# A single-expert unit ahead of each group of mixed units, an early first weight load, and filler products, in a two-layer diffusion backbone with grouped experts

## What is computed

```python
x = x + gate2 * moe_ffn(rmsnorm(x) * (1 + scale2) + shift2)

def moe_ffn(h, ...):
    s = sigmoid(h @ w_router)                 # 16 experts in 4 groups of 4
    # best group by the sum of its two best biased scores, then its two best experts
    gates = the two chosen scores, divided by their sum
    hid = silu(h @ w1[e]) * (h @ w3[e])       # 1024 -> 256, for the chosen experts
    return sum over chosen e of gates[e] * (hid @ w2[e])    # 256 -> 1024
```

## Time and profile before

| | us |
|---|---|
| median of 3 runs | 1187.36 (1186.56 to 1190.74) |
| the profiled execution | 1180.08, its span 1177.2 |
| TensorE busy in it | 1094.7 |
| VectorE, ACT, POOL busy | 522.6, 275.8, 212.2 |

### The profile page before, as it was taken

How to read it: one execution, slowest core, us unless ns; L and a number is a source line. 1 busy time by engine, 2 the same in 40 slices (tenths; PEclk the granted TensorE clock), 3 DMA queues, 4 the chain that set the end, 5 groups by cost and what they waited for, 6 DMA issues and landing times.

```text
span 1177.2 us, 14999 instructions
## 1 busy us (share of the span) xinstructions
PE 1094.7 (93%) x5084; PEld 569.2 (48%) x5084; DVE 522.6 (44%) x1291; ACT 275.8 (23%) x637; POOL 212.2 (18%) x297
## 2 busy tenths in 40 slices
PE   5999999899999799999899999989999988899985
PEld 3556766555444343345345576655544433234432
DVE  1133554776236542424351535478623563224236
ACT  2121121566011111111152112156601111111111
POOL 5027100101122310000363510010112231000022
PEclk9999899999999899999999999999999978999998
DMA  9587741795404899998565841179300489999834
GB/s 348 212 273 279 277 179 36 292 355 213 179 0 170 335 376 365 417 417 355 208 259 187 345 168 66 36 272 360 120 18 1 154 325 348 368 417 414 333 131 189
DMA packets 62842, 288.29 MB, mean 245 GB/s; under 512 B 9776, under 2 KB 10944, under 8 KB 46832
## 3 DMA queue, kind: packets, MB, share of 16 engines
q1 hardware_dynamic: 33344, 190.87, 42.4%
q0 software_dynamic: 22608, 77.70, 18.4%
q10 hardware_dynamic: 6816, 18.78, 4.2%
HBM read 237.96 MB, written 55.93 MB: 250 GB/s over the span
## 4 chain that ended last, share of the span: by engine, by line
PE 74%; DMA 11%; DVE 5%; POOL 4%; issue 3%; ACT 2%; SPq 1%; another core or an unknown queue 0%; ACTq 0%; POOLq 0%; DVEq 0%
PE ps L1797 14%; PE ps L1319 12%; PE ps L1620 12%; PE ps L1821 6%; DMA arena<-in_w 5%; PE ps L1554 3%; PE ps L1585 2%; PE ps L1254 2%; PE ps L1247 2%; PE ps L1565 2%; DMA bias_rows<-bias_tab 2%; PE ps L1855 1%; PE ps L1185 1%; DVE arena L2659 1%; PE ps L1230 1%
## 5 line engine op out<-in xcount | busy, mean ns | idle before, releaser
L1797 PE MATMUL ps<-arena 128*32 128x512 f32 (+1 forms) x1024 | 206.0, 616 | 10.5 <-DMA arena<-in_w 9.6
L1319 PE MATMUL ps<-arena 128*128 128x320 f32 x560 | 159.7, 439 | 2.9 <-DVE arena L2426 2.9
L1620 PE MATMUL ps<-arena 128*128 128x512 f32 x320 | 140.4, 594 | 2.4 <-issue 2.4
L1797 PEld LDWEIGHTS ps<-arena 128*32 128x32 f32 (+1 forms) x1024 | 74.7, 134 | 136.6 <-issue 135.1
L1319 PEld LDWEIGHTS ps<-arena 128*128 128x128 f32 x560 | 106.7, 193 | 47.0 <-DVE arena L2426 3.1
L2924 DVE COPY arena<-ps 128x512 f32<-128x512 f32 x28 | 19.4, 691 | 193.4 <-PE ps L1761 193.4
L1821 PE MATMUL ps<-arena 128*32 128x512 f32 (+1 forms) x512 | 101.6, 595 | 3.3 <-issue 3.3
L1620 PEld LDWEIGHTS ps<-arena 128*128 128x128 f32 x320 | 59.5, 190 | 74.6 <-issue 74.6
L1131 POOL DMA_DIRECT2D arena<-expert_in x36 | 18.8, 521 | 262.5 <-issue 262.5
L1821 PEld LDWEIGHTS ps<-arena 128*32 128x32 f32 (+1 forms) x512 | 34.3, 129 | 50.6 <-issue 50.6
L2169 ACT ACTIVATE arena<-ps 128x256 f32<-128x256 f32 x28 | 10.7, 383 | 186.9 <-PE ps L1797 186.9
(11 more groups left out here) (349 smaller groups left out, 1570.8 us busy)
## 6 DMA issues: line engine op xcount, KB each, us to landing
arena<-in_w SPq DMA_DIRECT2D x96, 1024.0 KB, 17.4
arena<-in_w_ada SPq DMA_DIRECT2D x40, 1024.0 KB, 6.9
expert_in<-arena POOLq DMA_DIRECT2D x2, 8192.0 KB, 32.1
arena<-in_w_t SPq DMA_DIRECT2D x10, 1024.0 KB, 10.0
arena<-in_w_ada_c SPq DMA_DIRECT2D x8, 1024.0 KB, 13.2
arena<-in_w_out SPq DMA_DIRECT2D x8, 1024.0 KB, 7.4
arena<-mod_rows POOLq DMA_DIRECT2D x16, 512.0 KB, 11.4
arena<-in_w_n SPq DMA_DIRECT2D x8, 928.0 KB, 9.3
```

What stands on the lines that cost most here:

```text
L1319: ins = mm(out[:, 0:HALF], lhs[:, k, :], rhs[:, k, :], start=(first and k == 0), stop=(last and k == 3), skip_group_check=True)
L1620: ins = mm(out[:, n * 512:(n + 1) * 512], yT[:, k, t * P:(t + 1) * P], w[k // 2][:, k % 2, n * 512:(n + 1) * 512], start=(k == 0), stop=(k ...
L1797: ins = mm(out[lo:lo + n, :], hsT[b][:, k, lo:lo + n], w[role][:, k, :], start=(k == 0), stop=(k == KD - 1), skip_group_check=True)
```

## The change

1. The order of units becomes (0), (1), (10), (2,5), (3,5), (4,5), (11), (6,9), (7,9), (8,9), (12), (13), (14), (15). Places change with it. Place 2 serves roles 10, 4, 9; place 3 roles 2, 11, 8, 13; place 0 roles 0, 5, 7, 14; place 1 roles 1, 3, 6, 12, 15. By the same sorting rule SP now issues up 10, up 2, up 5, down 10, up 3, down 2, down 5, up 4, down 3, up 11, down 4, up 6, up 9, down 11, up 7, down 6, down 9, up 8, down 7, up 12, down 8, up 13, down 12, down 13, and then the weights of roles 14 and 15.
2. The up part of place 2 moves from h2 to the space of xT. The first load (up 10) no longer waits for `tokens0` and the scatter; the second and all later ones do.
3. TensorE gets products whose results are overwritten: two ahead of the transposes of the last tile in layer 1, three ahead of the second rank product in layer 0, two between units 0 and 1 in both layers.
4. VectorE: the six operations that work out the role and the gate of each choice move from before the copy of `tokens0` into `rows_of_round`, behind the copy for unit 0, and the register load of the number of rounds moves behind the copy of `tokens0`. They use a tile of their own, `r_chosen`.

```diff
+    def mixed(low):
+        return [[(low + i, 0, LOW_CAP, 0), (low + 3, LOW_CAP, P - LOW_CAP, (P - LOW_CAP) * i)] for i in range(3)]
+    def single(*roles):
+        return [[(role, 0, P, 0)] for role in roles]
+    return single(0, 1, LAST_LOW) + mixed(2) + single(LAST_LOW + 1) + mixed(6) + single(*range(LAST_LOW + 2, NE))
-PLACE_OF = {0: 0, 1: 1, 2: 2, 5: 3, 3: 0, 4: 1, 6: 2, 9: 0, 7: 1, 8: 3, 10: 2, 11: 1, 12: 3, 13: 2, 14: 0, 15: 1}
+PLACE_OF = {0: 0, 1: 1, 10: 2, 2: 3, 5: 0, 3: 1, 4: 2, 11: 3, 6: 1, 9: 2, 7: 0, 8: 3, 12: 1, 13: 3, 14: 0, 15: 1}
...
-        up_at = [at_ring + SLOT, at_ring + 3 * SLOT, at_h + 2 * SLOT, at_h]
-        down_at = [at_ring, at_ring + 5 * SLOT, at_h + 4 * SLOT, at_up]
+        up_at = [at_ring + SLOT, at_ring + 3 * SLOT, at_y, at_h]
+        down_home = [view(at_ring, 2, D), view(at_ring + 5 * SLOT, 2, D), view(at_h + TL * D, 2, KD * N_TOK)[:, :, 0:D], view(at_up, 2, D)]
...
                     wait(sp, roles_ready.sem, roles_ready.at(l, 1))
-                    filled(sp, l, "tokens0")
-                    wait(sp, scattered.sem, scattered.at(l, 16 * 2 * TT))
...
-                        for load, role in WEIGHTS_ORDER:
+                        for n, (load, role) in enumerate(WEIGHTS_ORDER):
+                            if n == 1:
+                                filled(sp, l, "tokens0")
+                                wait(sp, scattered.sem, scattered.at(l, 16 * 2 * TT))
...
                 def mixed_columns(t):
                     out = acquire(pe, l, ("xT", t))
+                    if t == TL and l + 1 == DEPTH:
+                        for n in range(2):
+                            mm(out[:, n * 512:(n + 1) * 512], ones, xT[:, 0, 0:512], start=True, stop=True)
...
                     pe.wait_ge(ahead_used.sem, ahead_used.at(l, KD))
                     pe.sem_inc(psum_full, 1)
+                    out_0 = acquire(pe, l, "tokens0")
+                    for _ in range(3):
+                        mm(out_0[:, 0:512], ones, xT[:, 0, 0:512], start=True, stop=True)
...
                         for e in range(2):
+                            if e == 1:
+                                for _ in range(2):
+                                    mm(ps[:, 3 * BANK:4 * BANK], hsT[0][:, 0, :], hsT[0][:, 0:4, :], start=True, stop=True)
                             first_tokens(base, turn, e)
...
-                for of_expert, of_choice in ((r_role_row, r_role), (r_cap_of, r_cap)):
-                    link(V(r_t, r_sel, of_expert.unsqueeze(1).unsqueeze(1).broadcast_to((P, 2, TT, NE)), ALU.mult))
-                    link(dve.tensor_reduce(of_choice, r_t, AX.X, ALU.add))
...
-                link(dve.scalar_tensor_tensor(out=r_gate2, in0=r_role, scalar=float((NE - 1) * P), in1=gates,
-                                              op0=ALU.is_equal, op1=ALU.mult))
-                link(V(r_gate, r_gate2[:, 0], r_gate2[:, 1], ALU.add))
...
                 def rows_of_round(turn):
+                    for n, (of_expert, of_choice) in enumerate(((r_role_row, r_role), (r_cap_of, r_cap))):
+                        V(r_chosen, r_sel, of_expert.unsqueeze(1).unsqueeze(1).broadcast_to((P, 2, TT, NE)), ALU.mult)\
+                            .then_inc(back_chain, 1)
...
+                    V(r_gate, r_gate2[:, 0], r_gate2[:, 1], ALU.add).then_inc(back_chain, 1)
...
+                dve.tensor_copy(hs[:, 0, 512:1024], filled(dve, l, "tokens0")[:, 512:1024]).then_inc(first_high.sem, 1)
                 n_rounds = dve.value_load(rounds_i[0:1, 0:1], min_val=1, max_val=5)
-                dve.tensor_copy(hs[:, 0, 512:1024], filled(dve, l, "tokens0")[:, 512:1024]).then_inc(first_high.sem, 1)
```

More of the change, by code:

```diff
@@ L35 @@
 CREDIT = 2
-DVE_CHAIN = 171
+DVE_CHAIN = 165
 ROUNDS = N_TOK // P
@@ L496, in mixer_kernel @@
         r_cap_of = rcut(NE)
+        r_chosen = view(at_a + D, 2, TT, NE)
         r_role = rcut(2, TT)
@@ L1812, in down @@
                     for role, _, _, _ in EXPERT_UNITS[u]:
-                        w[role] = view(down_at[loaded(down_in, turn, role, 16)], 2, D)
+                        w[role] = down_home[loaded(down_in, turn, role, 16)]
                     pe.wait_ge(hidT_ready, base + u + 1)
@@ L2947, in rows_of_round @@
                 def rows_of_round(turn):
+                    for n, (of_expert, of_choice) in enumerate(((r_role_row, r_role), (r_cap_of, r_cap))):
+                        V(r_chosen, r_sel, of_expert.unsqueeze(1).unsqueeze(1).broadcast_to((P, 2, TT, NE)), ALU.mult)\
+                            .then_inc(back_chain, 1)
+                        dve.wait_ge(back_chain, turn * 16 + (2 * n + 1))
+                        dve.tensor_reduce(of_choice, r_chosen, AX.X, ALU.add).then_inc(back_chain, 1)
+                        dve.wait_ge(back_chain, turn * 16 + (2 * n + 2))
+                    dve.scalar_tensor_tensor(out=r_gate2, in0=r_role, scalar=float((NE - 1) * P), in1=gates,
+                                             op0=ALU.is_equal, op1=ALU.mult).then_inc(back_chain, 1)
+                    dve.wait_ge(back_chain, turn * 16 + 5)
+                    V(r_gate, r_gate2[:, 0], r_gate2[:, 1], ALU.add).then_inc(back_chain, 1)
                     role = r_role.rearrange("p a t -> p (a t)")
@@ L2954, in rows_of_round @@
                     dve.tensor_scalar(r_last, r_rel2, 1.0, None, ALU.add).then_inc(back_chain, 1)
-                    dve.wait_ge(back_chain, turn * 10 + 3)
+                    dve.wait_ge(back_chain, turn * 16 + 9)
                     dve.scalar_tensor_tensor(out=r_in, in0=r_rel, scalar=0.0, in1=r_in,
@@ L2959, in rows_of_round @@
                                              op0=ALU.is_equal, op1=ALU.mult).then_inc(back_chain, 1)
-                    dve.wait_ge(back_chain, turn * 10 + 5)
+                    dve.wait_ge(back_chain, turn * 16 + 11)
                     dve.scalar_tensor_tensor(out=r_in, in0=role, scalar=float((NE - 1) * P), in1=r_in,
@@ L2963, in rows_of_round @@
                     V(r_high, r_last[:, 0], r_last[:, 1], ALU.max).then_inc(back_chain, 1)
-                    dve.wait_ge(back_chain, turn * 10 + 7)
+                    dve.wait_ge(back_chain, turn * 16 + 13)
                     dve.scalar_tensor_tensor(out=r_at_row, in0=r_at_row, scalar=spare_row, in1=r_in,
@@ L2968, in rows_of_round @@
                     dve.tensor_scalar(r_high, r_high, 1.0, None, ALU.subtract).then_inc(back_chain, 1)
-                    dve.wait_ge(back_chain, turn * 10 + 10)
+                    dve.wait_ge(back_chain, turn * 16 + 16)
                     dve.tensor_scalar(back_i[:, :], r_at_row, spare_row, None, ALU.add).then_inc(back_ready, 1)
```

2 lines of the change are left out of this document (1 added, 1 removed).

## The result

The changed kernel takes 1166.16 us (median of 4 runs, 1165.7 to 1167.1), the kernel before 1186.96 us (4 runs, 1182.12 to 1190.74). The ratio is 0.9831, 95% interval 0.9807 to 0.9854: 20.8 us, or 1.7%, faster.

The account below looks back on a forecast made before the run. It took the kernel to be TensorE-bound, so only pauses and slow stretches could be won: layer 0 -0.6, layer 1 -6.1, late weights at unit 12 +1.4, sum -5.3 us off the 1187.36 us median: 1182.0 us, range 1170 to 1191.

Parts of the forecast that it names:

- the first part: Opening account of TensorE's expert stages: late weights cost layer 1 some 12.3 us, layer 0 only about 1.5.
- Layer 0: +0.9 - 1.5 = -0.6: Layer 0's sum: unit 1 starts 0.9 us later, 1.5 us lost to late weights goes away.
- part 1: Order of units: weight waits at units 2 and 5 go, unit 7 costs nothing, unit 12 adds 1.4 us in all.
- Rival D: Expert stages: the wait for weights only moves, to units 7 to 9; 1187 or 1188 us, chance 0.17.
- part 2: First load beside the scatter: scatter pushed back 5.9 and 5.0 us, unit 1 starts 0.9 and 4.7 us later.
- one to one: DMA queues: SP's weights and another queue alternate packet for packet, 58 beside 60; a weight packet takes 0.31 to 0.43 us.
- The scatter's queue ends near 406 and 965: Sign of being right: scatter's queue ends at these times in layers 0 and 1, SP's packets beside it.
- parts 4 and 5: TensorE's fillers and VectorE's moved operations: covered by pauses and the wait for expert 1's tokens, 0 us.
- B: Rival: early load starts later or loses against the scatter, which is hardly held up; -17 us, 1170 us, chance 0.22.
- C: Rival: token load becomes the stage's wait, landing in 10.2 us in both layers; +6.7 us, 1194 us, chance 0.13.
- my signs: Profile after: token waits in both layers, 3 to 6 us in layer 1; no weight waits at units 2 and 5.
- the 3 us mark for the total: Sign of being right: waits on weights in the up products fall from 9.6 us to under 3.

Follow-up runs that it names:

- e1: The kernel before, unchanged, run and profiled a second time: ratio 1.0003 to the kernel before.
- e9: The kernel before with ten filler products added between units 0 and 1 of each layer: 1176.03 us, ratio 0.9920 to the kernel before.
- e3: The kernel before with the seven filler products alone: ratio 0.9991 to the kernel before.
- e12: The kernel before with VectorE's move alone: ratio 0.9998 to the kernel before.
- e5: The kernel before with the new order of units and its places alone: ratio 0.9963 to the kernel before.
- e2: The changed kernel without all seven filler products: ratio 0.9828 to the kernel before.
- e10: The changed kernel without its fillers, with ten products added between units 0 and 1 of each layer: 1172.8 us, ratio 0.9894 to the kernel before.
- e6: The kernel before with the early load alone, in the old order: ratio 0.9895 to the kernel before.
- e7: The kernel before with new order and early load, without VectorE's move and fillers: ratio 0.9848 to the kernel before.
- e8: The changed kernel without fillers, with role 12 in place 0 and role 13 in place 1: ratio 0.9839 to the kernel before.
- e14: The kernel before with new order and early load, run again on another chip: 1162.96 us, ratio 0.9841 to the kernel before.
- e16: The changed kernel without fillers, run again: 1166.44 us, ratio 0.9856 to the kernel before.
- the square: Four kernels on one chip, all with the new order and no fillers, with or without early load and VectorE's move: 1162.96 to 1175.61 us.
- e13: The kernel before with the new order and places alone, run again: 1175.61 us, ratio 0.9953 to the kernel before.

## Why the prediction was right in sign and wrong in size

**The step that failed** is in the first part: "layer 0 only about 9.6 - 8.1 = 1.5 us", with what was built on it, "Layer 0: +0.9 - 1.5 = -0.6". It was one execution's figure taken for the kernel's; that this execution lay 7.28 us below the median was known, and I took the difference off the median without asking what it lacked. In that execution ACT's token load landed after 10.2 us, unit 1 of layer 0 started at 414.30 and not near 406 as in e1, and so TensorE was by chance as late as the weights: e9 without the products. Layer 0 typically loses as much as layer 1: 15.1 and 14.8 us in e1, 11.4 and 11.0 in e3, 13.1 and 12.3 in e12. I left some 10 to 14 us out, most of the 15.5 us between forecast and result. The row that could have told me was before me, and I took from it only the clock and the rate: DMA share 1.02 at 369 GB/s, with TensorE waiting. I priced single waits at single units, where the weights' queue over the whole stage set when unit 5 could start.

By e1 the sum comes out. Its waits on weights are 24.5 us, and its products behind them are slow by (8.77 - 7.07) + (8.92 - 7.07) + (8.93 - 7.07) = 5.4 us; after, 4.3 us of waits are left, and unit 1 of layer 1 adds 3.9 us of waiting and 2.0 of slow product: 24.5 + 5.4 - 4.3 - 5.9 = 19.7 us, against 20.8 by the medians and 18.6 between the spans of these two executions.

**Order (part 1).** That the waits of units 2 and 5 go is right. "Is it only moved, to unit 7 ... I cost it at nothing" is right for the whole change and wrong for the order alone: 4.33 and 6.90 us at unit 7 in e5. I had reckoned role 9's bytes at a free queue (8.5 us for 3 MB); its 2 MB up part alone took up to 22.5 us there, and up to 17.4 even in the changed kernel, whose 1.76 us at unit 7 of layer 0 are that. Rival D's wait at unit 7 is what the order alone shows, though not its time, and I gave the early load no part in the weights' queue at all. Unit 12: 0.7 us per layer taken, 0 to 2 as bounds; 1.19 and 1.40 measured, 2.6 in all where I had added 1.4.

**Early load (part 2).** It does push the tokens back, but by less than I said. SP's first load went out 2.2 and 2.0 us behind the end of the roles' instruction (1.4 taken). Its packets came some 3.6 us after that (1.7 taken), in layer 1 mostly behind the scatter. DMA queues in windows of 2 us, kernel after, layer 1 (packets, MB, share), first 952 to 954:

```profile
...
q1 hardware_dynamic: 21, 0.17, 20.3%
q0 software_dynamic: 201, 0.70, 86.2%
...
```

and 954 to 956:

```profile
...
q1 hardware_dynamic: 101, 0.83, 97.7%
q0 software_dynamic: 7, 0.02, 2.5%
...
```

The scatter's bulk is through at 954, with hardly a weight packet between. In layer 0 the two do mix, as I had reckoned: in each microsecond from 396 on queue 0 moves 49, 34, 21, 12, 4 and 3 packets (119 alone before) beside 28, 37, 47, 63, 50 and 51 weight packets. The "one to one" was read from two queues where there were three: in the windows of the earlier trace rows queue 0 moved 23 and 46 packets more.

Against before, ACT's token load comes 3.9 us later in layer 0 and 3.5 in layer 1 (402.22 + 2.9 - 401.2, and 959.68 + 5.65 - 961.86, where 2.9 and 5.65 are what the two executions are apart at the scatter's first transfer), not 5.9 and 5.0. It landed in 3.5 and 3.7 us, not 6.5, though role 2's load starts 0.6 us behind it in both layers, as I had said.

In all runs with the whole early load the landing goes with how far ahead of it the early load was issued: at 8.3 us or more (both layers of the changed kernel, layer 0 of e2 and e10, layer 1 of e6) it is 3.5 to 3.7 us, at 4.6 to 7.9 us (the other eleven stages of e2, e6, e7, e8, e10, e14 and e16) it is 4.2 to 9.9. The later the scatter's semaphore lets ACT go, the less is left of the early load beside the tokens, which fits these numbers; no run separates the two.

The tokens were there 29.6 and 29.5 us behind the scatter's first transfer, where I had put 34.6 and 33.9; without the early load it is 25.8 to 26.5 (e1 and e12). "The scatter's queue ends near 406 and 965" was wrong for its bulk in layer 1; of its last few packets it is nearly true (402 + 2.9 and 960 + 5.65). Unit 1 of layer 1 lost 0.9 us (4.7 said) and then took 9.07 (8.8 said).

**Fillers and VectorE (parts 4 and 5)** were costed at 0, and e2, e3, e12 and the square show 0. Unit 0 of layer 1 does start earlier, 3.5 us net of the offset, and the tokens' wait takes it up, as I said.

**The rivals.** B's number, 1170, was nearest, and its condition (the load loses against the scatter) is what the queues of layer 1 show; its sign came too, unit 1 of layer 1 before 972 (965.44, or 971.09 with the 5.65 us). But its sum too had 1.5 us for layer 0, so that it was nearest is in part luck. C didn't come: the tokens landed in 3.5 and 3.7 us, and the 9.9 and 7.7 us of e7 cost no time that shows. Of my signs, the waits of 3 to 6 us on tokens in layer 1, waits at unit 12 and none at units 2 and 5 came true; the wait on tokens in layer 0, nothing left but unit 12, and the 3 us mark for the total did not.

## What to carry to other kernels

Before pricing waits one by one, divide the span into stages and put TensorE's busy share beside the DMA share in each: where the DMA share is 1.0 and TensorE waits now and then, the bytes of the stage over its rate are the first estimate of its time, and moving 2 MB to where the DMA engines stand idle (here 12 us for two layers) was worth more than the order within it (4 to 6). One profile's list of waits is a sample: 9.6, 17.7, 19.4 and 24.5 us for kernels of one time (the first and the last for the very same kernel), so a second profile is worth more than a closer reading of the first. A stage's bound can be shown by adding work to the engine that seems to be it: if the time doesn't grow, it isn't, at the place where the work was added.

## What the runs showed of the hardware that was not expected

- 17 us of added TensorE work made the kernel 9.4 us faster (e9).
- The scatter's completion trails its bulk where weight packets stand beside it: in layer 1 after 954 the queue shows 7, 5 and 3 packets per 2 us, and ACT, which waits for its semaphore, issues at 959.68, 5.7 us later. Before, with no weights beside, the last heavy stretch ended near 960, 11 packets followed by 962, and ACT issued at 961.86, 2 us later. The delay differs from execution to execution of one kernel: ACT issues 27.4 and 22.3 us behind the scatter's first transfer in e2, 24.3 and 21.9 in e16. The Trainium skill (DMA: Bandwidth & Descriptors, Queues, rings and completion order) says that a DMA's semaphore increment lands only after every earlier write of that engine, across its queues; the trace agrees with it but doesn't separate it from the few late packets.
- The same pause is followed by the lower clock or not: the 40 records at 118 us, in code that no kernel here edits, took 14.03 us behind 2.94 us of idling in the first profile, 11.04 behind the same 2.94 in e1, which is the same kernel, and 11.03 behind 3.27 in the changed one. It is 3 us of difference between profiles that belongs to no edit.
- A token load of 512 KB landed in 3.4 to 10.2 us, by what was under way beside it. Without an early load it is 3.4 to 3.6 us where SP's first load goes out 0.7 us or more behind it, 4.2 and 4.0 at 0.16 us (layer 0 of e5 and e13), and 10.2 where that load went out 0.27 us ahead of it (layer 0 of the first profile, 402.26 against 402.53).
